# The weights' tile, and what lies behind it, 64 bytes further on in SBUF

## What is computed

```python
h = layer_norm(ALPHA * x + mixer(x))             # layer 0: gated short convolution, layer 1: causal pooling
r = relu(h @ mlp_w1[i])                          # 1024 -> 4096
f = (r * r) @ mlp_w2[i]                          # 4096 -> 1024
e = (p[i] @ ple_w[i]) * sigmoid(h @ ple_gate_w[i])
x = layer_norm(ALPHA * h + f + e)
```

## Time and profile before

| | |
|---|---|
| median of three runs | 2120.43 us (2119.01 to 2122.08) |
| the profiled execution | 2124.93 us, of which 2123.1 us from the first to the last instruction |
| PE (TensorE matmul) busy | 2112.3 us, 99%, 13221 instructions |
| PEld (weight load) busy | 2109.8 us, 99% |
| DVE, ACT, POOL busy | 1267.3, 823.3, 73.5 us |
| DMA | 179.68 MB, mean 85 GB/s |
| granted TensorE clock | 0.998 of 2.4 GHz |

### The profile page before, as it was taken

One profiled execution on the slowest core, in us unless ns is written; L12 is line 12 of the kernel. 1 busy time (PEld: TensorE's weight loads), 2 busy tenths in 40 slices (PEclk: granted clock), 3 DMA queues, 4 the chain that ended last, 5 costly groups with the idle time before them and its releaser, 6 DMA issues.

```text
span 2123.1 us, 31857 instructions
## 1 busy us (share of the span) xinstructions
PE 2112.3 (99%) x13221; PEld 2109.8 (99%) x13221; DVE 1267.3 (60%) x1892; ACT 823.3 (39%) x1288; POOL 73.5 (3%) x67
## 2 busy tenths in 40 slices
PE   9999999999999999999999999999999999999998
PEld 9999999999999999999999999999999999999998
DVE  5232357786454444444777877887866346544477
ACT  4221233653433322222543645555443224333345
POOL 0000000000000000000020002000300000000000
PEclk9999999999999999999999999999999999999999
DMA  4010231444222111111112343543123112112233
GB/s 174 30 59 30 69 129 47 129 133 133 67 84 96 50 49 41 42 59 41 60 61 80 107 133 126 169 138 120 61 77 104 56 50 72 62 66 80 70 100 132
DMA packets 53777, 179.68 MB, mean 85 GB/s; under 512 B 8080, under 2 KB 10512, under 8 KB 53648
## 3 DMA queue, kind: packets, MB, share of 16 engines
q1 hardware_dynamic: 50768, 177.33, 25.5%
q10 hardware_dynamic: 2880, 0.52, 0.1%
HBM read 173.36 MB, written 4.46 MB: 84 GB/s over the span
## 4 chain that ended last, share of the span: by engine, by line
PE 98%; ACT 1%; DVE 1%; issue 0%; DMA 0%; DVEq 0%; POOL 0%; ACTq 0%; POOLq 0%
PE ps L697 32%; PE ps L699 32%; PE ps L698 32%; ACT acc L955 0%; PE ps L862 0%; PE ps L722 0%; PE ps L726 0%; DMA w_raw<-w_stream 0%; PE ps L732 0%; DVE acc L1173 0%; PE ps L750 0%; PE ps L749 0%; ACT w_split L880 0%; DVE acc L1297 0%; DVE std L1213 0%
## 5 line engine op out<-in xcount | busy, mean ns | idle before, releaser
L697 PE MATMUL ps<-h_hi,w_split 128*128 128x352 f32 x2160 | 697.4, 323 | 1.6 <-ACT t L1005 0.7
L699 PE MATMUL ps<-h_hi,w_split 128*128 128x352 f32 x2160 | 692.5, 321 | 0.0
L698 PE MATMUL ps<-h_lo,w_split 128*128 128x352 f32 x2160 | 692.1, 320 | 0.0
L697 PE MATMUL ps<-r_hi,w_split 128*128 128x352 f32 x1634 | 527.0, 322 | 0.4 <-DVE acc L1297 0.4
L699 PE MATMUL ps<-r_hi,w_split 128*128 128x352 f32 x1634 | 524.0, 321 | 0.0
L698 PE MATMUL ps<-r_lo,w_split 128*128 128x352 f32 x1634 | 523.5, 320 | 0.0
L1297 DVE TENSOR_TENSOR acc<-acc,ps 128x352 f32<-128x352 f32 (+1 forms) x769 | 374.8, 518 | 134.6 <-PE ps L699 133.8
L616 DVE TENSOR_TENSOR w_split<-w_raw,w_split 128x1024 fp32r<-128x1024 f32 x291 | 357.7, 1251 | 111.6 <-ACT w_split L880 110.8
L697 PEld LDWEIGHTS ps<-h_hi,w_split 128*128 128x128 f32 x2160 | 405.0, 187 | 3.2 <-issue 1.8
L698 PEld LDWEIGHTS ps<-h_lo,w_split 128*128 128x128 f32 x2160 | 406.3, 188 | 0.0
L699 PEld LDWEIGHTS ps<-h_hi,w_split 128*128 128x128 f32 x2160 | 404.9, 187 | 0.0
(11 more groups left out here) (128 smaller groups left out, 1196.8 us busy)
## 6 DMA issues: line engine op xcount, KB each, us to landing
w_raw<-w_stream SPq DMA_DIRECT2D x315, 512.0 KB, 3.5
x_raw<-x_t SPq DMA_DIRECT2D x4, 704.0 KB, 7.8
y_t<-acc SPq DMA_DIRECT2D x4, 704.0 KB, 4.3
w_raw<-p_t SPq DMA_DIRECT2D x6, 352.0 KB, 2.9
y_t<-acc SPq DMA_DIRECT2D x3, 352.0 KB, 2.2
w_raw<-w_stream SPq DMA_DIRECT2D x3, 256.0 KB, 4.7
x_raw<-x_t SPq DMA_DIRECT2D x4, 176.0 KB, 3.7
x_raw<-x_t SPq DMA_DIRECT2D x2, 352.0 KB, 5.7
```

Source lines behind the costliest of these rows:

```text
L697: pe.matmul(out, wh, mov_h, start=first, stop=False)
L698: pe.matmul(out, wh, mov_l, start=False, stop=False)
L699: return pe.matmul(out, wl, mov_h, start=False, stop=last)
```

## The change

One line is added ahead of the place of `w_split`. It moves the cursor and the base `at7`, from which `u`, `gc` and `conv` are placed, by 64 bytes.

```diff
         hl, at7 = place("h_lo", big, F32R)
         xraw, _ = place("x_raw", big, F32, at6)
         squares, _ = place("ln_squares", big, F32, at6)
+        cursor[0], at7 = cursor[0] + 64, at7 + 64
         ws, _ = place("w_split", [P, 6, 2, U], F32R)
         UW = CH + PROMPT + CH + SAMPLE
```

## The result

The kernel after takes 2130.07 us (median of 6 runs, 2130.01 to 2130.82), the kernel before 2121.45 us beside it (6 runs, 2119.01 to 2123.82). The ratio on record is 1.0045, with an interval of 1.0033 to 1.0056 (the two medians by themselves give 1.0041): slower by some 0.4%, and clear of no change. The predicted 2120.5 us was for no change; the time lies in the range of 2107 to 2143 us, on rival B's side.

What follows compares the result with a forecast made beforehand. The prediction took TensorE as the bound, the number of matmuls by their start-to-start distance. Four terms of 0 summed to no change on the profiled 2124.9 us, 2120.5 us given as likeliest for the median, range 2107 to 2143 us.

Steps and rivals of the forecast that it cites:

- rival B: Every matmul slower because weight load and moving stream meet differently; +6.5 us, +22 us or +36 us; chance 0.35.
- the likeliest case: No effect of the weights' address, same levels in about the same stretches: 2120.5 us, own range 2117 to 2124 us.
- The bound: TensorE, busy 2112.3 of 2123.1 us: time is the number of matmuls by their start-to-start distance; four waits, 0.4 to 0.7 us.
- Step 1: About 13,040 matmuls with `w_split`, weight loads beginning 64 bytes past a multiple of 256: taken at zero.
- the ends: Limits for the weights' address effect: -1.5 to +2.5 ns a distance over 13,040 matmuls, -20 to +33 us.
- Step 2: Which distance level holds in which stretch: taken at 0, between -7 us (all low) and +22 us (all high).
- Steps 3 and 4: DVE and ACT operations on moved tiles, taken at nothing; loads into `w_raw`, taken at 0 with a 0.7 us bound.
- the middle level holds everywhere: All 13,040 matmuls at 160.0 ns against a mean of 159.5 ns: +6.5 us, 2127 us.
- all at the low level: The 3,160 matmuls at 161.1 ns go to 158.9 ns: -7 us, 2113 us.
- The first one: Sign that the stretches 463 to 1016 and 1561 to 1745 us still give 158.9 ns, matmul lengths 318 to 323.
- The sign for step 1: Prediction wrong if a window that TensorE fills has a distance not among the three of before.
- The last sign: Also wrong, with step 1 right, if the low level is hardly reached any more or covers the first stage too.

Runs made afterwards that it cites:

- e2_rest_only: Against the kernel before, `w_split` stayed put and `w_raw` and all tiles behind it moved 64 bytes: 2121.89 us, ratio 1.0003.
- e7_low_half_128: Against the kernel before, the weights' low halves were placed apart from the high halves, 128 bytes past a multiple of 256: 2118.12 us, ratio 0.9995.
- e1_weights_only: Against the kernel before, `w_split` with `u`, `gc`, `conv` moved 64 bytes, tiles behind it 256, keeping their address modulo 256: 2130.76 us, ratio 1.0044.
- e3_all_moved: Against the kernel before, all tiles, moving operands too, began 64 bytes further on: 2122.28 us, ratio 1.0006.

## Why the prediction was right or wrong

The range held the time, and the likeliest case didn't happen. The range ran from all matmuls at the low level to all at the high one, so that nearly any outcome of the levels would have fallen into it; that it held is no sign that the weights' address costs nothing.

- **The bound** was right. TensorE is full, and the distance between matmuls moved the time. (Its waits are five, not four: one of 1.1 us for POOL at the start belongs to them.)
- **Step 1, the weights' address, taken at zero**, is the step that failed. It was held at nothing, and its cost is the whole result. It was priced by the rows in which a load is alone the pace, and those still read 0.11 us in other layouts; but such a row can't show what two streams do to each other. The rows for that were the earlier trace rows, which the text had put down as the ends, -20 to +33 us. The cost is +5.3 us on the profiled execution, inside the ends.
- **Step 2, the levels**, was right in its rows and its prices: 158.9, 160.0 and 161.1 ns are the means of the windows before and after. It left out that an address can take away the choice.
- **Steps 3 and 4** (DVE and ACT, loads) were right: 525 and 526 ns, loads that land after 3.5 us, 7.4 us of waits for transfers, and `e2_rest_only` at 1.0003.
- **Rival B**, with a chance of 0.35, named the case: "if the middle level holds everywhere", +6.5 us. The mean is that of the middle level, though it comes by another beat, 1920 ns for twelve distances and not 960 for six. Its 2127 us should have been 2131: the 6.5 us belong to the profiled execution's 2124.9 us, because the level of each stretch is drawn anew in each execution, and only that execution's draw was known. Measured for the one that was profiled: 2130.14 us. For the median, before's draw was better than in its profile, so the loss is 8.6 us and not 5.2. The same holds for the other prices that were put on 2120.4 us: all at the low level is 2117 us and not 2113, and `e7_low_half_128`, nearly all at that level, measured 2118.1.
- **The signs.** The first one decided: the stretches from 463 to 1016 and from 1561 to 1745 us no longer give 158.9 ns. The sign for step 1, a distance that isn't among the three of before, didn't appear although the step was wrong; it was too narrow, since an address can also bring the middle number everywhere. The last sign, a low level that is hardly reached any more, did appear; the text had put it beside a right step 1, and `e1_weights_only` and `e3_all_moved` show that it comes of the weights' place.
- **The page's rules.** The Trainium skill's "TensorE: Matmul & The Clock Gate", section "Step-by-step: what each phase is for", says that loading the next weights takes no read bandwidth in SBUF from the running matmul. In this trace the load isn't without effect on the stream beside it: moving the loads by 32 bytes, and nothing else that TensorE touches but the norms' tiles by 256, took the distance from 158.9 to 162.2 ns. Whether it is bandwidth that they share no run here shows. The 149 ns from the same page's "Back-to-back issue gap" are no measure for this kernel: the section gives the formula for a single matmul by itself, and says that in a stream of loads and matmuls both set the spacing. Of the extra transaction in "DMA: Bandwidth & Descriptors" of the Trainium skill, section "How a descriptor splits into AXI transactions", no cost is seen: the loads of the kernel after land after 3.5 us as before.

What stays open is why: which part of the chip takes turns, and how. The runs show that the distance between the addresses of load and stream is what counts, not the start of either, and that it acts with the other engines at rest. They don't give a rule by which a layout's number could be worked out.

## What to carry to other kernels

Where TensorE is full and each matmul brings its own weights, measure the distance from start to start by window: one level or several at the same shape and clock is a hint that place and start have a hand in it. A shift of the stationary tile against the moving one is a change like any other and cost 1.8% here with 32 bytes; keep it fixed when something else is compared, since a tile put ahead of it moves it. And price a change of level from the profiled execution's own time, not from the median.

## What was not expected of the hardware

- Matmuls of 352 columns with a load each come mostly at 158.3, 158.9, 160.0, 161.1, 161.6, 162.2, 163.3 or 166.7 ns, at a granted clock of 1.00; only the grid of layouts has steady numbers between these. In the kernel before, six distances at 158.9, 160.0 and 161.1 ns are 953.3, 960.0 and 966.7 ns: steps of 6.7 ns, the time of 16 columns at 2.4 GHz. 158.3 and 161.6 ns lie half a step beside, and with weights at 64 bytes only twelve distances together are constant, 1920 ns.
- A level, once reached, can hold for thousands of matmuls (553 us in one window), and an idle time of under a microsecond, or two matmuls of another tile, can change it. By the start times, all stretches of before at 158.9 ns have the first matmul of a pair of blocks at the same place on one grid of 6.7 ns, through idle times and stretches at other levels, with a slow drift of some 3 ns in 1.8 ms. What keeps that grid no run here shows.
- With one kind of block and weights 128 bytes off it, the same stretch read 158.3 or 166.7 ns in one kernel, by its start, and 158.3 seven times in 7 in another, on another chip.
